# The first mixer's product tiles in another order, and half of the modulation vectors computed inside the first experts

## What is computed

```python
cond = silu(c)
for i in range(2):
    mod = cond @ w_ada[i] + b_ada[i]            # 1024 -> 6 * 1024, once for each layer
    sh1, sc1, g1, sh2, sc2, g2 = split(mod, 6)
    h = rms_norm(x, norm_g[i, 0]) * (1 + sc1) + sh1
    y = hgrn2_mixer(h, ...) if i == 0 else rglru_mixer(h, ...)
    x = x + g1 * y
    h = rms_norm(x, norm_g[i, 1]) * (1 + sc2) + sh2
    x = x + g2 * peer_ffn(h, ...)               # 16384 experts, all weights streamed

# hgrn2_mixer, layer 0 only
q, f_fw, f_bw, v, g = split(h @ w_in, 5)        # five times 1024 columns
f = lb + (1 - lb) * sigmoid(f_logit)            # for each direction; k = 1 - f
o = scan(q, k_fw, v, log f_fw) + reversed scan(q, k_bw, v, log f_bw)
o = rms_norm(o, norm_g) * silu(g)
return o @ w_out
```

## Time and profile before

| | us |
|---|---|
| median of 3 runs (3310.99 to 3312.83) | 3312.6 |
| the profiled execution's own time | 3312.08 |
| its span in the trace | 3310.4 |

### The profile page before, as it was taken

How to read it: one execution, slowest core, us unless ns; L and a number is a source line. 1 busy time by engine, 2 the same in 40 slices (tenths; PEclk the granted TensorE clock), 3 DMA queues, 4 the chain that set the end, 5 groups by cost and what they waited for, 6 DMA issues and landing times.

```text
span 3310.4 us, 65113 instructions
## 1 busy us (share of the span) xinstructions
PE 3036.7 (92%) x22954; PEld 2911.9 (88%) x22954; DVE 2245.7 (68%) x4716; ACT 1601.9 (48%) x3283; POOL 65.4 (2%) x113
## 2 busy tenths in 40 slices
PE   4987799999999999899999999998968589988898
PEld 4877699999999998799999999998957479976898
DVE  5639359888877774459888877777554348764586
ACT  1110256777644443556777644444532237462484
POOL 2210000000000000000000000000000000000000
PEclk9979799999999999899999999999979599997999
DMA  8940155444455553355444455554500045531453
GB/s 322 410 193 1 59 177 185 153 148 160 141 184 186 187 184 128 117 173 183 153 152 156 148 189 186 187 184 145 171 1 23 0 133 183 172 109 58 140 178 127
DMA packets 137756, 503.33 MB, mean 152 GB/s; under 512 B 15328, under 2 KB 15456, under 8 KB 137344
## 3 DMA queue, kind: packets, MB, share of 16 engines
q1 hardware_dynamic: 122544, 445.57, 40.3%
q0 software_dynamic: 15056, 55.65, 4.3%
HBM read 499.05 MB, written 2.10 MB: 151 GB/s over the span
## 4 chain that ended last, share of the span: by engine, by line
PE 78%; DVE 6%; ACT 4%; issue 2%; DVEq 0%; ACTq 0%
PE PB L483 11%; PE PB L485 11%; PE PB L484 11%; PE PA L485 9%; PE PA L483 9%; PE PA L484 9%; PE PB L473 4%; PE PA L659 4%; DVE w_low L1922 1%; PE PA L785 1%; PE PB L785 1%; PE PA L982 1%; PE PB L556 1%; PE PB L873 1%; DVE BIG L1948 1%
## 5 line engine op out<-in xcount | busy, mean ns | idle before, releaser
L1019 ACT ACTIVATE w_high<-ring 128x512 fp32r<-128x512 f32 x1484 | 927.5, 630 | 952.8 <-PE PA L485 478.2
L1922 DVE TENSOR_TENSOR w_low<-ring,w_high 128x512 fp32r<-128x512 f32 x1484 | 1015.6, 692 | 448.2 <-ACT w_high L1019 424.7
L483 PE MATMUL PB<-h_high,w_low 128*128 128x256 f32 x3536 | 1020.9, 289 | 47.9 <-DVE h_low L1610 36.9
L485 PE MATMUL PB<-h_high,w_high 128*128 128x256 f32 x3536 | 1002.5, 284 | 0.0
L484 PE MATMUL PB<-h_low,w_high 128*128 128x256 f32 x3536 | 1000.7, 283 | 0.0
L483 PEld LDWEIGHTS PB<-h_high,w_low 128*128 128x128 f32 x3536 | 683.1, 193 | 62.0 <-issue 39.4
L483 PE MATMUL PA<-a_high,w_low 128*128 128x256 f32 x2400 | 676.4, 282 | 10.1 <-DVE a_low L1931 10.1
L485 PE MATMUL PA<-a_high,w_high 128*128 128x256 f32 x2400 | 675.7, 282 | 0.0
L484 PEld LDWEIGHTS PB<-h_low,w_high 128*128 128x128 f32 x3536 | 675.3, 191 | 0.0
L485 PEld LDWEIGHTS PB<-h_high,w_high 128*128 128x128 f32 x3536 | 674.1, 191 | 0.0
L484 PE MATMUL PA<-a_low,w_high 128*128 128x256 f32 x2400 | 673.4, 281 | 0.0
(11 more groups left out here) (327 smaller groups left out, 2909.7 us busy)
## 6 DMA issues: line engine op xcount, KB each, us to landing
ring<-tiles SPq DMA_DIRECT2D x842, 512.0 KB, 3.3
BIG<-ada POOLq DMA_DIRECT2D x96, 512.0 KB, 14.0
BIG<-skew POOLq DMA_DIRECT2D x4, 512.0 KB, 4.3
X<-x SPq DMA_DIRECT2D x1, 1024.0 KB, 5.7
skew<-BIG POOLq DMA_DIRECT2D x1, 1024.0 KB, 7.0
out<-X SPq DMA_DIRECT2D x4, 256.0 KB, 2.0
con<-consts SPq DMA_DIRECT2D x1, 853.0 KB, 8.7
BIG<-masks POOLq DMA_DIRECT2D x1, 768.0 KB, 6.2
```

The source lines that it names most:

```text
L483: mm(dst, lhs_l, high, start=start, stop=False, skip_group_check=True)
L485: return mm(dst, lhs_h, high, start=False, stop=stop, skip_group_check=True)
L1019: fn(tile_half(w_high, s, b), ring[:, at:at + HALF], ACT.Identity).then_inc(sem("high_ready"), 1)
L1922: tt(tile_half(w_low, s, b), ring[:, at:at + HALF], tile_half(w_high, s, b).bitcast(F32), ALU.subtract).then_inc(sem("low_ready"), 1)
```

## The change

The tiles of `hg_in` are stored in the order f, f, q, v, g, and BIG's places for q and f are exchanged to suit. ACT applies Sigmoid to the 16 f tiles and Silu to the 8 g tiles as it empties their slots; the three whole-buffer activations go. Groups 2 to 5 (the rest of layer 0) are summed in the mixer as before; PE adds them up after 24 tiles, before the v and g tiles, and DVE makes the gates after that, each way when its tiles are taken. Groups 6 to 11 (layer 1) move into the first experts' down tiles: POOL loads them once down tile 31 has been split, into the freed first 32T columns; DVE does one of their tiles behind two of every three down tiles from 38 to 109, in straight code there instead of the loop; PE adds them up into PB behind down tile 124; DVE's `modulate` follows its last tile. The wait for `gate_silu` moves from `head_norm` to the callers that need it.

```diff
-        HG = dict(chunks=DC, heads=HG_HEADS, q=big(0, DC * T), v=big(24 * T, DC * T),
+        HG = dict(chunks=DC, heads=HG_HEADS, q=big(16 * T, DC * T), v=big(24 * T, DC * T),
...
-                  ways=[dict(f=big(8 * T, DC * T), k=big(48 * T, DC * T), q=big(64 * T, DC * T),
+                  ways=[dict(f=big(0, DC * T), k=big(48 * T, DC * T), q=big(64 * T, DC * T),
...
-                        dict(f=big(16 * T, DC * T), k=big(56 * T, DC * T), q=big(72 * T, DC * T),
+                        dict(f=big(8 * T, DC * T), k=big(56 * T, DC * T), q=big(72 * T, DC * T),
...
-        ADA_RING, ADA_SUMS = big(40 * T, DC * TILE), big(72 * T, 12 * D)
+        LATER, ADA_FROM, ADA_TILES = 6, 38, 9 * DC
+
+        def ada_ring(layer, k):
+            return big((0 if layer else 40 * T) + k * TILE, TILE)
+
+        def ada_sums(layer, at, n):
+            return BIG[:, bass.ds(at + (32 * T - LATER * D if layer else 72 * T), n)]
...
-            def ada(first, last):
+            def ada(first, last, dst=PA):
                 pe.wait_ge(sem("ada_sums_ready"), last)
                 for m in range(first * DC, last * DC):
-                    ins = mm(PA[:, m:m + 1], ADA_SUMS[:, m * P:(m + 1) * P], c("ones", 0, 1),
+                    ins = mm(dst[:, m:m + 1], ada_sums(first // LATER, m * P, P), c("ones", 0, 1),
...
                     for j in range(1, 5):
                         down(j, it)
+                if layer == 0:
+                    pe.wait_ge(sem("up_taken"), c0 + NKEYS)
+                    ada(LATER, 12, PB)
                 for j in range(4 * steps + 1, NKEYS):
                     down(j)
...
-            linear("hg_in", H, sem("h_ready"))
-            ada(2, 12)
+            linear("hg_in", H, sem("h_ready"), 0, 3 * DC)
+            ada(2, LATER)
+            linear("hg_in", H, None, 3 * DC)
             all_taken("hg_in")
...
-            evacuate("hg_in", big(0, 40 * T))
-            all_taken("hg_in")
-            fn(HG_G, HG_G, ACT.Silu).then_inc(sem("gate_silu"), 1)
-            act.wait_ge(sem("ada_used"), 12 * DC)
-            for way in HG["ways"]:
-                fn(way["f"], way["f"], ACT.Sigmoid).then_inc(sem("gate_sigmoid"), 1)
+            evacuate("hg_in", big(0, 16 * T), ACT.Sigmoid, 0, 2 * DC)
+            evacuate("hg_in", big(16 * T, 16 * T), ACT.Identity, 2 * DC, 4 * DC)
+            evacuate("hg_in", HG_G, ACT.Silu, 4 * DC, 5 * DC)
+            act.wait_ge(sem("ada_psum"), 2)
...
+            def ada_tile(g, k, layer):
+                dve.wait_ge(ada_loaded[k], (g + 1) * 16)
+                dst, cond = ada_sums(layer, g * D, D), coef[:, k:k + 1]
+                if k:
+                    dve.wait_ge(sem("ada_used"), g * DC + k)
+                    ins = stt(dst, ada_ring(layer, k), cond, dst, ALU.mult, ALU.add)
+                else:
+                    ins = ts(dst, ada_ring(layer, k), cond, None, ALU.mult)
+                ins.then_inc(sem("ada_used"), 1)
+                if k == DC - 1:
+                    dve.wait_ge(sem("ada_used"), g * DC + DC)
+                    v.tensor_copy(stat[:, 14:15], big(32 * T if layer else 72 * T, 1)).then_inc(sem("ada_sums_ready"), 1)
...
-                spans(dve, late, (2, NKEYS))
+                if layer:
+                    spans(dve, late, (2, NKEYS))
+                else:
+                    spans(dve, late, (2, ADA_FROM))
+                    for j in range(ADA_FROM, ADA_FROM + ADA_TILES):
+                        late(j, 0)
+                        i, rest = divmod(j - ADA_FROM, 3)
+                        if rest < 2:
+                            ada_tile(LATER + (2 * i + rest) // DC, (2 * i + rest) % DC, 1)
+                    spans(dve, late, (ADA_FROM + ADA_TILES, NKEYS))
+                    modulate(LATER, 12, PB)
                 add_sums(run, modulation(layer, 1, 2))
...
-            ada(2, 12)
-            all_taken("hg_in")
-            modulate(2, 12)
-            for way in HG["ways"]:
-                dve.wait_ge(sem("gate_sigmoid"), w.up(sem("gate_sigmoid")))
+            ada(2, LATER)
+            modulate(2, LATER)
+            for d, way in enumerate(HG["ways"]):
+                dve.wait_ge(taken, (d + 1) * DC)
...
+            dve.wait_ge(taken, 3 * DC)
             decay_attention(HG)
             v.tensor_copy(HG_MIX, PA[:, :]).then_inc(sem("heads_ready"), 1)
             dve.wait_ge(sem("heads_ready"), w.up(sem("heads_ready")))
+            all_taken("hg_in")
             head_norm(HG_MIX, HG_HEADS, lambda h: p("hg_norm_g", h, 1), HG_G)\
...
-            with pool.Fori(1, 12) as g:
+            with pool.Fori(1, LATER) as g:
                 for k in range(DC):
                     pool.wait_ge(sem("ada_used"), g * DC + (k - DC + 1))
                     load_ada(k, g)
+            pool.wait_ge(sem("gated_ready"), 32)
+            for k in range(DC):
+                load_ada(k, LATER, 1)
+            with pool.Fori(LATER + 1, 12) as g:
+                for k in range(DC):
+                    pool.wait_ge(sem("ada_used"), g * DC + (k - DC + 1))
+                    load_ada(k, g, 1)
...
-    put("hg_in", tiles_of(a["hg_w_in"][0]))
+    hg = tiles_of(a["hg_w_in"][0])
+    put("hg_in", np.concatenate([hg[DC:3 * DC], hg[:DC], hg[3 * DC:]]))
```

More of the change, by code:

```diff
@@ L456, in loop, with linear @@
                     body(i, 0)
-            def linear(name, src, pairs=None):
+            def linear(name, src, pairs=None, first=0, last=None):
                 r0, n = STREAM_AT[name]
+                last = n if last is None else last
                 q0 = product_at[name][0]
@@ L475, in body @@
                     ins.then_inc(tile_done, 1)
-                loop(n, body, peel=1 if q0 == 0 else 0)
+                loop(last - first, lambda i, it: body(first + i, it), peel=1 if q0 + first == 0 else 0)
             def passes(dst, k, b, at, high, low, start, stop):
@@ L1562, in add_sums, with modulate @@
                     add_chunk(m, PA[:, m * T:(m + 1) * T], gate).then_inc(sem("x_added"), 1)
+            def ada_tile(g, k, layer):
[10 more added lines that the diff above has]
+                    v.tensor_copy(stat[:, 14:15], big(32 * T if layer else 72 * T, 1)).then_inc(sem("ada_sums_ready"), 1)
             def ada(first, last):
-                def part(g):
+                with dve.Fori(first, last) as g:
                     for k in range(DC):
[L1568 to L1583, removed]
+                        ada_tile(g, k, 0)
+            def modulate(first, last, src=PA):
                 dve.wait_ge(sem("ada_psum"), w.up(sem("ada_psum")))
                 cols = slice(first * DC, last * DC)
-                tt(mod[:, cols], PA[:, cols], p("b_ada", first * DC, (last - first) * DC), ALU.add)\
+                tt(mod[:, cols], src[:, cols], p("b_ada", first * DC, (last - first) * DC), ALU.add)\
                     .then_inc(sem("dve_step"), 1)
@@ L1647, in head_norm @@
                 inverse_heads(n)
-                dve.wait_ge(sem("gate_silu"), w.up(sem("gate_silu")))
                 for i in range(n // 2):
@@ L2149, in even_mixer @@
                 ins.then_inc(sem("carry_ready"), 1)
+                dve.wait_ge(sem("gate_silu"), w.up(sem("gate_silu")))
                 head_norm(e["mix"][:, 0:6 * T], 6, lambda h: p("gdn_norm_w"), e["z"])\
@@ L2348, in _, with load_ada @@
             w = Tally()
-            def load_ada(k, g):
-                pool.dma_start(ADA_RING[:, k * TILE:(k + 1) * TILE], ada_in[g, k])\
-                    .then_inc(ada_loaded[k], 16)
+            def load_ada(k, g, layer=0):
+                pool.dma_start(ada_ring(layer, k), ada_in[g, k]).then_inc(ada_loaded[k], 16)
             for k in range(DC):
                 load_ada(k, 0)
-            with pool.Fori(1, 12) as g:
+            with pool.Fori(1, LATER) as g:
                 for k in range(DC):
```

## The result

| | before | after |
|---|---|---|
| median, us | 3311.8 (4 runs, 3310.7 to 3312.8) | 3291.4 (4 runs, 3286.3 to 3293.0) |
| span of the profiled execution | 3310.4 | 3289.5 |

The ratio is 0.9934, interval 0.9922 to 0.9946: faster by 20.4 us. The forecast was 3291.0.

What follows compares the result with a forecast made beforehand. PE was taken as the bound, with 63.7 us of hardly any useful PE work in the mixer's tail. Terms -44.5 + 19.9 + 3.0 = -21.6 us gave 3291.0 us against a median of 3312.6, range 3277 to 3303.

Steps and rivals of the forecast that it cites:

- What bounds the kernel: PE carries most of the chain; a change counts where PE stands still, runs slowly or gets more to do.
- Step 1: Mixer's tail: 64 records moved between product tiles cost a 13.0 us detour, gates get hidden, masking starts 44.5 us earlier.
- Step 2: Behind down tile 124: PE's 96 added records and the return to dense work cost 19.9 us.
- Rival 1: Both PE detours: the clock stays full through one-column matmuls, total 3276.8 us; chance 13%.
- Step 3: Down tiles 38 to 109: DVE's 48 added weight tiles cost 3 us, chosen between 0.6 and 14.4.
- Rival 2: Down tiles: DVE becomes the bound, each insertion shifts PE by its own length, 60.8 us, total 3348.8; chance 7%.
- Costed at nothing: Down tiles: POOL's 48 loads beside the ring's cost nothing, with landing times of 6.8 us (ring) and 14.2 (POOL) allowed.
- Rival 3: Down tiles: ring tiles come late beside POOL's loads, 5.7 us once or more, about 3297 to 3303; chance 11%.
- Rival 4: Mixer's tail: shortened less because something else held the attention, every 10 us that stay make 3301; chance 4%.

Runs made afterwards that it cites:

- Experiment 3: The changed kernel with the mixer's tiles, activations and gates as before, layer 1's vectors still moved to the experts: 3296.32 us, ratio 0.9945.
- experiments 2 and 6: 128 columns of ones in place of one in PE's adding-up: 2 on the changed kernel, 3271.34 us; 6 on the kernel before, 3295.36 us.
- experiment 4: The changed kernel with layer 1's folds on DVE cut to one column of 1024, loads and waits kept: 3291.93 us, ratio 0.9933.
- experiment 5: The changed kernel with one fold behind each of down tiles 38 to 85, not two in every three of 38 to 109: 3296.61 us, ratio 0.9951.
- experiment 1: The changed kernel run again, unedited: 3286.24 us, ratio 0.9922.

## Why the prediction was right

**What bounds the kernel** stood: apart from the drift of unchanged code, only stretches where PE idled or was given more work moved.

**Step 1** (44.5 us forecast, 45.45 measured). The product ended at 149.40 + 58.55 = 207.95 instead of 195.7, so the detour was 12.25 us against 13.0: 64 records 9.14 (10.4 forecast) and 3.1 for going back (2.6 forecast). The records were cheaper because the clock stayed up longer: a mean of 0.78 over 9.3 us is 5.2 us at full, not the 4.0 taken from an idle PE; and at full clock a one-column record took 0.112 us, not 0.117. Gates were hidden, as costed, and the last slot, transposes and scores took 213.99 - 207.98 = 6.0 of the 6.2 forecast. Experiment 3 shows that the term has two sources; the forecast didn't separate them.

**Step 2** (19.9, measured 18.6). The 96 records took 16.2 (17.3 forecast), for the same two reasons, and going back took 2.4 (2.6 forecast). `modulate` at 1225.75 stood ahead of the residual's wait and cost nothing. That one-column records let a full clock fall was an inference in the forecast; the windows of this kernel show it, and experiments 2 and 6 show what 128 columns do instead. Rival 1, a clock that stays full, is false for one column and true for 128: its 3276.8 compares with 3271.3 and 3272.3, which also have the gain at groups 0 and 1 that the rival did not count.

The Trainium skill, TensorE: Matmul & The Clock Gate, section on the HAM clock gate, puts the clock down to PE's recent busyness. With gapless streams of equal weights and count, 160 records at 0.50 with one column and 0.91 mean with 128, these runs say that the busy share which the profile shows for PE does not by itself tell the clock: the trace disagrees with the rule if it is read that way.

**Step 3** (3 us, measured 2.4). That DVE's time is the cost was right; experiment 4 shows it. The amount owes something to luck, since 3 was a choice between 0.6 and 14.4, and the form is neither of these two. The forecast set an insertion's whole 1.3 us against 0.7 us of slack. But the insertion stands ahead of DVE's wait for w_high (0.71 a tile), which takes up most of it. What reaches a_low is 1.88 + 1.20 - 2.83 = 0.25 us for each full fold. The lead of a_low goes from 0.60 us to 0.36 and 0.13 with two folds, and the tile without one gives it back. By PE's starts of the tiles, 12 of the 24 pairs cost nothing, six 0.1 us each and six 0.3 us each; the last are those that end a group, where the copy is added. So below DVE's throughput (8.0 to 8.3 of 8.5 us) only a used-up lead is paid, and above it, in experiment 5, the excess. Rival 2, 60.8 us, is false, at one fold per tile as well: DVE is the bound there, but a fold shifts PE by 0.24 us and not by its own length. In the changed kernel DVE still waits for w_high 14.1 us in 32 times over 208 us, against 88.0 in 124 over 350 us before.

**Costed at nothing.** The loads: ring tiles landed in 4.4 us in the folds' stretch, POOL's in 4.1, against the 6.8 and 14.2 that the forecast allowed. Around the first eight loads (925 to 955 us) it was 6.1 and 9.4, and the down tiles 2 to 38 took 101.8 us, as before. Experiment 4 lost nothing with all of the loads. Rival 3 is false. Rival 4 is false too: masking began 0.9 us ahead of the forecast.

**The total** agrees to 0.4 us, closer than the terms earn. Unchanged code contributed +3.4, which no step had, and it ranges over some 7 us between executions of one kernel (1060.5 and 1067.3 in the last third alone). A forecast of 3287 would have been as good; experiment 1's median is 3286.2.

## What to carry to other kernels

Look for work that sits at half clock between two dense stretches, and ask first whether it must be a thin matmul: widening it to 128 columns was one line here and worth 15 us on the changed kernel, 17 on the one before. For work put on an engine with gaps, sum the demand over a period instead of pricing each insertion by its length: above the period the excess is lost (3.07 of 2.83 us lost 0.24 a tile, 9.4 in all), and just below it only what the lead doesn't cover (at most 8.3 of 8.5 us lost 2.4). Read the lead, and ask what the engine waits for behind the insertion. And read a small gain from the stretches it should appear in, since code behind it can drift by as much as the gain.

## What the hardware showed that was not expected

- The clock fell under one-column fp32 matmuls without a gap (64 records 9.14 us at a mean of 0.78, then 0.50 in dense tiles behind). Under 128-column ones with the same weights it stayed at 1.00 (7.31 us) and came up from half (160 records in 20.74 us against 34.30, 0.91 in the mean over 208 to 230).
- At the same clock the two widths cost the same: 0.112 us from record to record at full, 0.213 at half, for one column as for 128.
- Time lost after such a stream is as real as in it: 3.1 us of the detour's 12.25 fell on dense product tiles.
- The same stretch with 30 PE records took 15.5 us at a mean clock of 0.55 or 12.8 at 0.73, and PE's busy time makes up 2.6 of the 2.7 us; the last third of the kernel differed by 6.8 us, 6.3 of them PE's busy time.
